# Second attention in pair steps, with half-array products and unpadded queries

## Chip, cores and metric

The kernel runs on one core of a Trainium2 chip. The metric is the device time of one launch in microseconds (us). TensorE is called PE, VectorE DVE, ScalarE ACT, GpSimd POOL and SyncE SP, as the profile calls them; PEld is PE's weight load.

## The reference, cut to what matters

Two layers run over 544 tokens: a prompt of 512 and a sample of 32 new tokens with a cache of 256. In each layer:

```
h = rms_norm(x, norm1)
a_q, a_k, a_v, b_q, b_k, b_v, i_q, i_k, i_w = split(h @ w_in)
o_a = stick_breaking(a_q, a_k, a_v)                      # 8 heads of 64, strictly causal
b_q = rms_norm(b_q, q_norm); b_k = rms_norm(b_k, k_norm) # per head
# keys of each query: the top k of an indexer's scores (i_q, i_k, i_w)
logits = b_q @ b_k^T / 8 + bias[pos]; not selected: -inf
o_b = softmax(logits) @ b_v                              # 8 heads of 64
x = x + concat(o_a, o_b) @ w_out
x = x + conv_ffn(rms_norm(x, norm2))
```

All in float32. For the 512 prompt queries the second attention works in tiles: a tile is one head and one block of 128 queries (b = 0 to 3), with 128(b + 1) keys.

## The kernel before

Activations lie transposed in SBUF, with 128 features of a matrix on the partitions and the 544 tokens along the row, so a column block of 128 of `w_in` is a *unit*, and a unit of the second attention holds two heads (a *pair* p = 0 to 3): head 2p on partitions 0 to 63, head 2p+1 on 64 to 127. A projection of a unit, `("G", kind, p, half)`, is cut into two halves of 24 products each (L1148, L1149, L1152: high and low parts of both operands). Its result stands in PSUM in one of two slots that are used in turn, and the next but one user of the slots waits until DVE or ACT has emptied it.

All engines walk one list of steps, made by `layer_steps`, `a_phase` and `b_phase`, and each engine takes from a step what is its own, in order. The names: G a half projection; E its result scaled and stored by DVE; S, N, Y, M, W the root-mean-square norm of bq and bk (ACT squares, PE adds over a head, DVE stores the mean, ACT does a logarithm and an exponential, DVE three operations and the write of q or k); T a transpose back to rows for an output; C the split of the next weights (ACT copies the high part, L868, POOL subtracts for the low part, L1660); TOPK one round of the top-k on DVE; IDX the indexer; AZ, AP, AS, AX, AW the first attention for one head; ASZ to ASV the same for the sample; O the split of an attention output for `w_out`.

The second attention (`b_phase`) takes 34 tiles one by one, head after head, then two of the sample. For tile i:

- BL: PE forms the logits in bank i % 2 of `a_ps` (L1341) and adds the mask of excluded keys by a product with the identity (L1342). It waits until ACT has read tile i-2. DVE adds the bias and takes the maximum (L1637), and negates it (L1639).
- BX: ACT takes the exponential and the sum (L1001).
- In the next BL: DVE takes the reciprocal (L1643), POOL scales the tile (L1674).
- BT: PE turns the tile by 128 x 128 blocks (L1351), ACT copies it out (L1017, L1019). All tiles use bank 2, so each waits for the copy of the one before.
- BV: after both heads of a pair, PE multiplies by the values (L672) into bank 3, and DVE copies to `o_t`.

The half projections and norms of the next pair stand between these steps by the table in `b_phase`, in some steps two, in many none.

A query is stored twice over in `q_pad`: for each head of the pair all 128 partitions, those of the other head being zero, so that a product with the pair's keys on 128 partitions gives one head. The writes are two DVE operations on 64 partitions each (L1464 for bq, L1488 for iq and aq). The indexer alone takes its products from 64 partitions (L1225). The last value unit, bv 3, is projected and turned at the end of the first attention.

Of the kernel before, what the change touches and what calls it, by code (L numbers as in the profile page):

```python
# [36 lines left out]
P = 128  # L37
# [81 lines left out]
B_TILES = [(h, b) for h in range(NH) for b in range(QB)] + [("s", 0), ("s", 1)]  # L119


def a_phase():
# [33 lines left out]
    bq, bk, bv = product("bq", 0), product("bk", 0), product("bv", 3)  # L156
    s += [("AZ", 6), ("AP", 6), ("AW", 2)] + turn + [bq[0], bq[1], ("E", "bq", 0), ("S", "bq", 0), ("AS", 6), ("AX", 6)]
    s += [("N", "bq", 0), ("Y", "bq", 0), bk[0], ("M", "bq", 0), ("W", "bq", 0), ("AZ", 7), ("AP", 7), bk[1], bv[0]]
    s += [("E", "bk", 0), ("S", "bk", 0), ("TOPK", 1), ("AS", 7), ("AX", 7), ("N", "bk", 0), ("Y", "bk", 0), ("TOPK", 1)]
    s += [("ASZ",), ("AW", 3), bv[1], ("ASP",), ("E", "bv", 3), ("ASS",), ("M", "bk", 0), ("W", "bk", 0), product("bq", 1)[0], ("ASV",), ("T", "bv", 3)]  # L160
# [3 lines left out]
def b_phase():  # L164

    extra = {i: [] for i in range(len(B_TILES) + 2)}
    late = {i: [] for i in range(len(B_TILES) + 2)}
    for p in range(1, PAIRS):  # L170
        i = 2 * QB * (p - 1) - 1
        halves = product("bq", p)
        if p > 1:
            late[i - 1] += [halves[0]]
        extra[i + 1] += [halves[1], ("E", "bq", p)]
        late[i + 1] += [("S", "bq", p)]
        late[i + 2] += [("N", "bq", p)]
        halves = product("bk", p)
        extra[i + 3] += [halves[0], ("Y", "bq", p)]
        extra[i + 3] += [("M", "bq", p)]  # L180
        extra[i + 4] += [("W", "bq", p), halves[1], ("E", "bk", p)]
        late[i + 4] += [("S", "bk", p)]
        late[i + 5] += [("N", "bk", p)]
        extra[i + 6] += [("Y", "bk", p)]
        extra[i + 6] += [("M", "bk", p)]
        extra[i + 7] += [("W", "bk", p)]
        extra[i + 8] += [("T", "bk", p)]
    extra[1] += [("T", "bk", 0)]
    n = len(B_TILES)
    for i in range(9):  # L190
        late[2 * i + 1] += [("TOPK", 1)]
    for j in range(KT // 2):
        extra[25 + j] += [("O", j)]
    extra[n - 1] += [("G", "wo", 0, 0)]
    extra[n] += [("G", "wo", 1, 0)]
    s = []
    for i in range(n + 2):
        if i <= n:
            s += [("BL", i)]
        s += extra[i]  # L200
        if i >= 3 and B_TILES[i - 3][1] == QB - 1 and B_TILES[i - 3][0] % 2:
            s += [("BV", B_TILES[i - 3][0] // 2)]
        if i >= 2:
            s += [("BT", i - 2)]
# [1514 lines left out]
```

## Time and profile before

| what | value |
|---|---|
| median of 3 runs | 1718.21 us (1717.36 to 1719.4) |
| the profiled execution's own time | 1717.34 us |
| its span, first to last instruction | 1715.5 us |
| mean granted PE clock | 0.982 of full |
| PE busy | 1606.1 us, 94% |
| DVE / ACT / POOL busy | 986.9 / 685.5 / 640.8 us (58% / 40% / 37%) |

Per layer, the second attention takes from 294.6 to 418.7 us in the first layer and from 1128.4 to 1252.5 us in the second.

PE's products are pipelined: the printed duration of one contains its way through the array, so that what a product costs in a row of them is the distance between two starts. Float32 products go in two passes, so one product shows as x2.

### The profile page before, as it was taken

What the parts mean: (1) busy time and instruction counts of PE and PEld (TensorE: products, weight loads), DVE (VectorE), ACT (ScalarE), POOL (GpSimd) and SP (SyncE); (2) the same over time, 40 slices, a digit from 0 to 9 for tenths busy, and PEclk for the clock granted to TensorE, in tenths of its full rate; (3) what the DMA queues carried; (4) which work ended last, traced back from release to release, by engine and by line L of the source; (5) the groups of instructions that cost most, each with busy time, mean ns of one, the idle gap of its engine ahead of it and who ended that gap; (6) DMA issues with size and microseconds to landing.
All of it is one profiled execution on the core that took longest, in us unless ns stands there. A gap on an engine that the chain in (4) does not pass through costs nothing.

```text
span 1715.5 us, 29957 instructions
## 1 busy us (share of the span) xinstructions
PE 1606.1 (94%) x11762; PEld 1475.9 (86%) x11762; DVE 986.9 (58%) x1823; ACT 685.5 (40%) x1296; POOL 640.8 (37%) x346
## 2 busy tenths in 40 slices
PE   5899999888999999999989899988789999999998
PEld 4678887666999999999987888876589999999998
DVE  6566766763756436616766666666556661663361
ACT  3333454444344324414433245534434441442342
POOL 4223331332734433433552323223345334434332
PEclk9899999998999999999999999999989999999999
DMA  6222212110322223233233231121012333333323
GB/s 184 68 78 82 70 50 64 51 50 1 89 85 87 87 87 87 87 89 91 74 89 98 65 96 48 47 70 51 20 50 78 95 87 87 87 87 87 86 82 97
DMA packets 242179, 131.43 MB, mean 77 GB/s; under 512 B 10303, under 2 KB 236591, under 8 KB 242039
## 3 DMA queue, kind: packets, MB, share of 16 engines
q1 hardware_dynamic: 242038, 129.52, 26.6%
q8 instruction: 93, 1.52, 0.4%
q14 instruction: 48, 0.39, 0.1%
HBM read 117.59 MB, written 11.62 MB: 75 GB/s over the span
## 4 chain that ended last, share of the span: by engine, by line
PE 70%; DVE 14%; ACT 6%; issue 3%; DVEq 3%; POOL 2%; ACTq 1%; DMA 0%; SPq 0%
PE g_ps L1148 13%; PE g_ps L1149 12%; PE g_ps L1152 12%; PE a_ps L1149 7%; PE a_ps L1148 7%; PE a_ps L1152 7%; DVE score L718 1%; ACT work L961 1%; PE a_ps L672 1%; POOL w_lo L1660 1%; PE a_ps L1238 1%; DVE score L1582 1%; DVE top L715 1%; PE a_ps L1225 1%; PE g_ps L1187 1%
## 5 line engine op out<-in xcount | busy, mean ns | idle before, releaser
L1660 POOL TENSOR_TENSOR w_lo<-raw,w_hi 128x1024 fp32r<-128x1024 f32 (+2 forms) x210 | 504.4, 2402 | 780.7 <-ACT w_hi L868 780.7
L1148 PE MATMUL g_ps<-h_hi,w_hi 128*128 128x272 f32 (+1 forms) x1632 | 454.0, 296 | 17.1 <-DVEq L1541 11.2
L1149 PE MATMUL g_ps<-h_lo,w_hi 128*128 128x272 f32 (+1 forms) x1632 | 443.6, 290 | 0.0
L868 ACT ACTIVATE w_hi<-raw 128x1024 fp32r<-128x1024 f32 (+2 forms) x210 | 217.4, 1035 | 502.9 <-PE g_ps L1152 371.2
L1152 PE MATMUL g_ps<-h_hi,w_lo 128*128 128x272 f32 (+1 forms) x1632 | 340.3, 290 | 0.0
L1148 PEld LDWEIGHTS g_ps<-h_hi,w_hi 128*128 128x128 f32 (+1 forms) x1632 | 309.1, 189 | 30.9 <-DVEq L1541 12.7
L1149 PEld LDWEIGHTS g_ps<-h_lo,w_hi 128*128 128x128 f32 (+1 forms) x1632 | 308.8, 189 | 0.9 <-issue 0.5
L1550 DVE SCALAR_TENSOR_TENSOR wts<-work,par,wts 128x546 f32<-128x546 f32 x176 | 201.2, 1143 | 100.0 <-ACT wts L1043 92.5
L1152 PEld LDWEIGHTS g_ps<-h_hi,w_lo 128*128 128x128 f32 (+1 forms) x1632 | 256.7, 189 | 0.0
L1148 PE MATMUL a_ps<-h_hi,w_hi 128*128 128x272 f32 x704 | 190.4, 288 | 0.0
L1149 PE MATMUL a_ps<-h_lo,w_hi 128*128 128x272 f32 x704 | 190.1, 288 | 0.0
L1152 PE MATMUL a_ps<-h_hi,w_lo 128*128 128x272 f32 x704 | 146.0, 288 | 0.0
L1148 PEld LDWEIGHTS a_ps<-h_hi,w_hi 128*128 128x128 f32 x704 | 132.6, 188 | 0.0
L1149 PEld LDWEIGHTS a_ps<-h_lo,w_hi 128*128 128x128 f32 x704 | 132.4, 188 | 0.0
L1152 PEld LDWEIGHTS a_ps<-h_hi,w_lo 128*128 128x128 f32 x704 | 110.0, 188 | 0.0
L1148 PE MATMUL g_ps<-act_hi,w_hi 128*128 128x272 f32 x364 | 99.3, 291 | 5.1 <-DVEq L1563 3.7
L1043 ACT ACTIVATE wts<-work,par 128x546 f32<-128x546 f32 x88 | 74.4, 845 | 61.1 <-DVEq L627 59.0
L1149 PE MATMUL g_ps<-act_lo,w_hi 128*128 128x272 f32 x364 | 98.2, 289 | 0.0
L1674 POOL TENSOR_SCALAR prob<-prob,stat 128x128 f32<-128x128 f32 (+2 forms) x68 | 47.8, 703 | 121.3 <-DVE stat L1643 121.3
L1148 PE MATMUL a_ps<-act_hi,w_hi 128*128 128x272 f32 x340 | 92.2, 289 | 0.9 <-POOL w_lo L1660 0.9
L1149 PE MATMUL a_ps<-act_lo,w_hi 128*128 128x272 f32 x340 | 91.7, 289 | 0.0
L1527 DVE TENSOR_TENSOR x_t<-x_t,g_ps 128x544 f32<-128x544 f32 x41 | 29.6, 721 | 107.4 <-PE g_ps L1152 106.7
(245 smaller groups left out, 2887.2 us busy)
## 6 DMA issues: line engine op xcount, KB each, us to landing
raw<-in_w_up SPq DMA_DIRECT2D x88, 512.0 KB, 3.8
raw<-in_w_in SPq DMA_DIRECT2D x56, 512.0 KB, 3.9
raw<-in_w_down SPq DMA_DIRECT2D x32, 512.0 KB, 3.7
raw<-in_w_out SPq DMA_DIRECT2D x16, 512.0 KB, 3.8
raw<-in_w_down SPq DMA_DIRECT2D x16, 384.0 KB, 3.4
x_nat<-in_x_prompt SPq DMA_DIRECT2D x4, 512.0 KB, 6.4
strip<-bias_line SPq DMA_DIRECT2D x8, 256.0 KB
out_p_av<-v_nat SPq DMA_DIRECT2D x4, 512.0 KB, 5.5
```

The lines of the kernel that those rows point to most:

```text
L672: mm = pe.matmul(a_ps[3][d, c * P:SEQ], v_nat[:, c, p * P + e * HD:p * P + (e + 1) * HD], pair_weights(w, e, c), start=(c == 0), stop=(c = ...
L715: dve.max(top8[0:n, i, :], s)
L718: dve.match_replace(s, top8[0:n, i, :], s, TAKEN)
L868: act.activation(w_hi[:, n % SPLIT, 0:kt, 0:c], raw[:, n % RAW, 0:kt, 0:c], ACT.Copy).then_inc(hi_done, 1)
L1043: act.activation(cbuf[kind], ubuf[kind][:, 2:U], ACT.Identity, bias=par[:, 3, col:col + 1], scale=par[:, 2, col:col + 1]).then_inc(c_tap.s ...
L1148: pe.matmul(g[0:c, a, 0:HALF], w_hi[:, s, j, 0:c], xh[:, mov], start=(j == 0), stop=False)
L1149: pe.matmul(g[0:c, a, 0:HALF], w_hi[:, s, j, 0:c], xl[:, mov], start=False, stop=False)
L1152: mm = pe.matmul(g[0:c, a, 0:HALF], w_lo[:, s, j, 0:c], xh[:, mov], start=False, stop=(j == kt - 1))
L1527: dve.tensor_tensor(halves(x_t[:, m, :]), halves(x_t[:, m, :]), g, ALU.add)
L1550: dve.scalar_tensor_tensor(c, u[:, tap:tap + U - 2], par[:, tap, col:col + 1], c, ALU.mult, ALU.add)
L1660: pool.tensor_tensor(w_lo[:, s, 0:kt, 0:c], raw[:, n % RAW, 0:kt, 0:c], w_hi[:, s, 0:kt, 0:c].bitcast(F32), ALU.subtract).then_inc(lo_done, 1)
L1674: pool.tensor_scalar(prob[:, i % 2, 0:w], prob[:, i % 2, 0:w], stat[:, i % 4, 3:4], 1.0, ALU.mult, ALU.mult).then_inc(b_nrm.sem, 1)
```

## The change

- `B_TILES` is ordered pair, block, head, and `b_phase` takes two tiles (both heads of a pair, one block) in a step: 16 prompt steps and one for the sample, plus one that ends it. One step holds at most one half projection.
- BL issues both heads' products from 64 partitions each, one behind the other (head 2p from the lower, head 2p+1 from the upper half of the array), then both masks. It waits until ACT has read both tiles of the step before.
- The reciprocal is one DVE operation for two tiles, in a step BR of its own, which POOL's two scalings follow.
- BT of a step turns both tiles behind the projection of the next step. Small tiles (b < 2) share bank 2 of `a_ps`; of large ones the first takes bank 2 and the second bank 3. `prob` has four tiles.
- `q_pad` is replaced by `q_t`, without zeros: one DVE operation on 128 partitions in place of two on 64. AZ reads 64 partitions and issues its four masks behind its four products.
- The projection of bv 3 and its turn move from the end of the first attention to steps 11 to 13 of the second. In their place stand the second half of bq 1, its E and S, and the first half of bk 1.

```diff
-B_TILES = [(h, b) for h in range(NH) for b in range(QB)] + [("s", 0), ("s", 1)]
+B_TILES = [(2 * p + e, b) for p in range(PAIRS) for b in range(QB) for e in range(2)] + [("s", 0), ("s", 1)]
...
-    s += [("ASZ",), ("AW", 3), bv[1], ("ASP",), ("E", "bv", 3), ("ASS",), ("M", "bk", 0), ("W", "bk", 0), product("bq", 1)[0], ("ASV",), ("T", "bv", 3)]
+    s += [("ASZ",), ("AW", 3), bq1[1], ("ASP",), ("ASS",), ("M", "bk", 0), ("W", "bk", 0), ("E", "bq", 1), ("S", "bq", 1), product("bk", 1)[0], ("ASV",)]
...
+    for q in range(PAIRS - 1):
+        p, j = q + 1, QB * q
+        k = product("bk", p)
+        first[j] += [("N", "bq", p), ("BR", j), ("Y", "bq", p), ("M", "bq", p)]
+        half[j] += [k[0]] if q else []
+        after[j] += [("W", "bq", p)]
+        first[j + 1] += [("BR", j + 1)]
+        half[j + 1] += [k[1], ("E", "bk", p)]
+        after[j + 1] += [("S", "bk", p)]
+        first[j + 2] += [("N", "bk", p), ("BR", j + 2), ("Y", "bk", p), ("M", "bk", p)]
+        first[j + 3] += [("T", "bk", p - 1), ("BR", j + 3), ("W", "bk", p)]
+        if p < PAIRS - 1:
+            later = product("bq", p + 1)
+            half[j + 2] += [later[0]]
+            half[j + 3] += [later[1], ("E", "bq", p + 1)]
+            after[j + 3] += [("S", "bq", p + 1)]
...
+    half[last - 1] += [value[0]]
+    half[last] += [value[1], ("E", "bv", PAIRS - 1)]
+    first[last] += [("T", "bk", PAIRS - 1)]
+    first[last + 1] += [("T", "bv", PAIRS - 1)]
+    half[last + 1] += [("G", "wo", 0, 0)]
+    half[last + 3] += [("G", "wo", 1, 0)]
+    for j in range(last, n):
+        first[j] += [("BR", j)]
+    for j in range(9):
+        after[j] += [("TOPK", 1)]
     for j in range(KT // 2):
-        extra[25 + j] += [("O", j)]
+        after[9 + j // 2] += [("O", j)]
     s = []
-    for i in range(n + 2):
...
+    for j in range(n + 1):
+        if j < n:
+            s += [("BL", j), ("BX", 2 * j), ("BX", 2 * j + 1)]
+        s += first[j] + half[j]
+        if j >= 2 and B_TILES[2 * j - 4][1] == QB - 1:
+            s += [("BV", (j - 2) // QB)]
+        if j:
+            s += [("BT", 2 * j - 2), ("BT", 2 * j - 1)]
+        s += after[j]
     s += [("BV", "s")]
...
-        q_pad = sb("q_pad", [P, 2, 2, TOK])
+        q_t = sb("q_t", [P, 2, TOK])
...
-                    ks = k_t[:, k_slot("ak", p), :]
+                    r = slice(e * HD, (e + 1) * HD)
+                    ks, q = k_t[r, k_slot("ak", p), :], q_t[r, q_slot("aq", p), :]
...
+                        for e in range(2):
+                            r = slice(e * HD, (e + 1) * HD)
+                            pe.matmul(a_ps[e][:, 0:w], q_t[r, q_slot("bq", p), b * P:(b + 1) * P], k_t[r, k_slot("bk", p), 0:w], start=True, stop=False)
+                        for e in range(2):
+                            pe.matmul(a_ps[e][:, 0:w], ident_b, excl[:, WOFF[b]:WOFF[b] + w], start=False, stop=True).then_inc(bl_full.sem, 1)
...
-                        for e in range(2):
-                            r = slice(e * HD, (e + 1) * HD)
-                            dve.scalar_tensor_tensor(halves(q_pad[r, q_slot(kind, p), e, :]), g[r], HD ** -0.5, halves(rstd[r, :]), ALU.mult, ALU.mult)
+                        dve.scalar_tensor_tensor(halves(q_t[:, q_slot(kind, p), :]), g, HD ** -0.5, halves(rstd[:]), ALU.mult, ALU.mult)
...
+                elif k == "BR":
+                    j = st[1]
+                    dve.wait_ge(b_exp.sem, b_exp.at(l, btiles[2 * j + 1]))
+                    c = 2 * (j % 2)
+                    dve.reciprocal(stat[:, c:c + 2, 3:4], stat[:, c:c + 2, 2:3]).then_inc(b_rcp.sem, 1)
```

First place: PE at the seam of the two attentions. Before, from the end of the sample's running sums (L1306) on: the first half of bq 1, the sample's values (L1314), the turn of bv 3 (L1198), and the first tile of the second attention (L1341).

```order
L1306 MATMUL a_ps<-work,cr 32x256
L1148 MATMUL g_ps<-h_hi,w_hi 128x272 [waits lo_done,g_free1]
...
L1314 MATMUL a_ps<-wts,vsa 128x64 [waits o_out,a_w]
L1314 MATMUL a_ps<-wts,vsa 128x64 x11
L1198 MATMUL g_ps<-cf,o_t 128x128 [waits e_done,g_free0]
...
L1341 MATMUL a_ps<-k_t,q_pad 128x128 [waits r_done,a_w]
L1342 MATMUL a_ps<-excl,cb 128x128
```

Now, in the changed program (L1315 is the old L1306, L1154 a projection, here the first half of bk 1, L1323 the sample's values, L1352 and L1354 the products and masks of a tile, L1193 the norm's product):

```order
L1315 MATMUL a_ps<-work,cr 32x256
L1154 MATMUL g_ps<-h_hi,w_hi 128x272 [waits lo_done,g_free1]
...
L1323 MATMUL a_ps<-wts,vsa 128x64 [waits o_out,a_w]
L1323 MATMUL a_ps<-wts,vsa 128x64 x11
L1352 MATMUL a_ps<-k_t,q_t 128x128 [waits r_done,a_w]
L1352 MATMUL a_ps<-k_t,q_t 128x128
L1354 MATMUL a_ps<-excl,cb 128x128 x2
L1193 MATMUL g_ps<-sq,cf 128x272 [waits sq_done,g_free0]
```

The turn of bv 3 has left; the wait on `g_free1` was for the emptying of bv 3 and is now for that of bq 1, which DVE does behind M and W of bk 0.

Second place: DVE in step 4, the first of the second group of four steps (L1647 and L1649 are the maximum with its read-out and the negation, L1435 N, L1654 the reciprocals, L1463 to L1470 M, L1479 and L1487 W of bq 2, L719 and L722 a round of the top-k).

```order
L1647 ISA a_ps,stat<-a_ps,strip 128x128 [waits b_nrm,bl_full]
L1647 ISA stat 128x1
L1649 TENSOR_SCALAR stat<-stat 128x1
...
L1435 TENSOR_SCALAR va<-g_ps 128x544 [waits g_full]
L1654 RECIPROCAL stat<-stat 128x2 [waits b_exp]
L1463 SCALAR_TENSOR_TENSOR va<-va,vb 128x544 [waits y_done]
L1465 TENSOR_TENSOR va<-va,vb 128x544
L1470 SCALAR_TENSOR_TENSOR vb<-va,vb 128x544
L1479 SCALAR_TENSOR_TENSOR q_t<-nraw,qk_gain,vb 128x544 [waits bl_full]
L1487 COPY q_smp<-q_t 64x32 x2
L719 MAX top<-score 32x8
L722 MATCH_REPLACE score<-top,score 32x288
```

Both tiles' maxima now come first in a step, and everything for the norms and the top-k stands behind the reciprocals, which wait for the exponentials of the same step.

## Rows read from the trace of the kernel before

**Rows 1.** The page: the span in 40 slices, tenths PE was busy, and its granted clock.
```profile
PE   5899999888999999999989899988789999999998
...
PEclk9899999998999999999999999999989999999999
```

**Rows 2.** Stages of layer 0: us, each engine's busy us (instructions), clock, DMA share, GB/s.
```profile
294.60:322.40 27.80, 23.41 (x153) 19.06 (x152) 19.57 (x57) 12.83 (x33) 9.01 (x8) 1.00 0.30 89
322.40:352.90 30.50, 25.93 (x172) 20.43 (x171) 21.37 (x62) 13.99 (x37) 9.86 (x10) 1.00 0.15 45
352.90:383.00 30.10, 23.80 (x148) 18.06 (x146) 19.77 (x58) 14.00 (x37) 10.58 (x11) 0.95 0.16 45
383.00:418.70 35.70, 30.93 (x172) 20.93 (x171) 11.99 (x48) 14.90 (x46) 8.04 (x12) 0.88 0.03 9
```

**Rows 3.** Timeline (start us, us, engine line op): a full-array tile; the indexer's half-array products.
```profile
305.21 1.02 PE L1341 MATMUL a_ps<-k_t,q_pad 128*128 128x512 f32 x2
306.07 0.38 PE L1342 MATMUL a_ps<-excl,cb 128*128 128x512 bf16 x1
...
74.09 1.13 PE L1225 MATMUL a_ps<-ik_t,q_pad 64*128 64x512 f32 x4 [0.47 <-ACT prob L953]
```

**Rows 4.** Timeline, PE: full array, half array, full array again.
```profile
71.92 0.41 PE L1152 MATMUL g_ps<-h_hi,w_lo 128*128 128x272 f32 x2
72.27 1.35 PE L1225 MATMUL a_ps<-ik_t,q_pad 64*128 64x256 f32 x8
...
75.15 0.68 PE L1225 MATMUL a_ps<-iks_t,q_pad 64*32 64x288 f32 x4
75.75 0.39 PE L1148 MATMUL g_ps<-h_hi,w_hi 128*128 128x272 f32 x1
```

**Rows 5.** Timeline, PE: AZ for a head, its first product and mask, and what follows.
```profile
159.31 1.02 PE L1238 MATMUL a_ps<-q_pad,k_t 128*128 128x512 f32 x2
160.16 0.22 PE L1239 MATMUL a_ps<-cb 128*128 128x128 bf16 x1
...
161.82 0.37 PE L1148 MATMUL g_ps<-h_hi,w_hi 128*128 128x272 f32 x1
```

**Rows 6.** Timeline, PE and DVE: the seam of the two attentions.
```profile
286.61 0.61 PE L1306 MATMUL a_ps<-work,cr 32*32 32x256 f32 x2
...
284.54 2.59 DVE L1446 SCALAR_TENSOR_TENSOR va<-va,vb 128x544 f32<-128x544 f32 x1 [0.28 <-issue]
...
289.77 0.18 DVE L1477 COPY ksb_t<-k_t 128x32 f32<-128x32 f32 x1
```

**Rows 7.** Timeline, DVE: a top-k round, two maxima, the write of a query pair.
```profile
302.41 0.45 DVE L715 MAX8 top<-score 32x8 f32<-32x288 f32 x1 [0.21 <-issue]
...
303.56 0.57 DVE L1637 CUSTOM_DVE_ANT_0 a_ps<-a_ps,strip 128x384 f32<-128x384 f32 x1
...
306.94 0.70 DVE L1637 CUSTOM_DVE_ANT_0 a_ps<-a_ps,strip 128x512 f32<-128x512 f32 x1
...
307.92 1.79 DVE L1464 SCALAR_TENSOR_TENSOR q_pad<-nraw,qk_gain,vb 64x544 f32<-64x544 f32 x2
```

**Rows 8.** Timeline, DVE and ACT: an operation of M, a weight copy, an exponential.
```profile
346.28 0.72 DVE L1446 SCALAR_TENSOR_TENSOR va<-va,vb 128x544 f32<-128x544 f32 x1 [0.36 <-ACT vb L904]
...
340.20 1.06 ACT L868 ACTIVATE w_hi<-raw 128x1024 fp32r<-128x1024 f32 x1 [3.31 <-PE g_ps L1152]
...
341.43 0.68 ACT L1001 ACTIVATE prob<-a_ps,stat 128x512 f32<-128x512 f32 x1
```

**Rows 9.** Timeline, DVE: a query write of the indexer.
```profile
59.18 1.46 DVE L1488 SCALAR_TENSOR_TENSOR q_pad<-g_ps,rstd 64x544 f32<-64x544 f32 x2 [7.04 <-PE g_ps L1152]
```

**Rows 10.** Timeline, PE: a turn at either clock, and the last values of the sample.
```profile
352.08 0.63 PE L1198 MATMUL g_ps<-cf,k_t 128*128 128x128 f32 x4 [0.68 <-DVEq L1478]
...
381.48 1.09 PE L1198 MATMUL g_ps<-cf,k_t 128*128 128x128 f32 x4 [2.34 <-DVEq L1478]
...
412.88 5.76 PE L1365 MATMUL a_ps<-wts,vsb 128*128 128x64 f32 x24 [0.62 <-ACT wts L1010]
```

More of the change, by code:

```diff
@@ L169, in b_phase @@
[L169 to L191, printed above, removed]
+    n = len(B_TILES) // 2
+    first, half, after = ({j: [] for j in range(n + 1)} for _ in range(3))
+    for q in range(PAIRS - 1):
[14 more added lines that the diff above has]
+            after[j + 3] += [("S", "bq", p + 1)]
@@ L192, in b_phase @@
+    last = QB * (PAIRS - 1)
+    value = product("bv", PAIRS - 1)
+    half[last - 1] += [value[0]]
[8 more added lines that the diff above has]
+        after[j] += [("TOPK", 1)]
     for j in range(KT // 2):
-        extra[25 + j] += [("O", j)]
@@ L1224, in _ @@
                             keys = ik_t[r, 0:w] if b < QB else iks_t[r, 0:w]
-                            pe.matmul(a_ps[i % 4][0:nq, 0:w], q_pad[r, q_slot("iq", p), e, q0:q0 + nq], keys, start=True, stop=True).then_inc(i_full.sem, 1)
+                            pe.matmul(a_ps[i % 4][0:nq, 0:w], q_t[r, q_slot("iq", p), q0:q0 + nq], keys, start=True, stop=True).then_inc(i_full.sem, 1)
                 elif k == "AZ":
@@ new lines, in _ @@
+                    if pair[0][0] == "s":
+                        pe.wait_ge(kc_done.sem, kc_done.at(l, "b"))
+                        pe.wait_ge(tk_done.sem, tk_done.at(l, "s"))
+                        for half in range(2):
+                            z = a_ps[half][:, 0:w]
+                            for r in range(2):
+                                p = 2 * half + r
+                                pe.matmul(z[r * 64:(r + 1) * 64, :], q_smp[:, p, :, :], ks_t["b"][:, p, :], start=True, stop=False, skip_group_check=True)
+                            pe.matmul(z, rep_b[0:DEC, :], excl_s[:], start=False, stop=True, skip_group_check=True).then_inc(bl_full.sem, 1)
+                    else:
+                        p = pair[0][0] // 2
+                        if b == 0:
+                            pe.wait_ge(r_done.sem, r_done.at(l, ("bk", p)))
+                        for e in range(2):
[3 more added lines that the diff above has]
+                            pe.matmul(a_ps[e][:, 0:w], ident_b, excl[:, WOFF[b]:WOFF[b] + w], start=False, stop=True).then_inc(bl_full.sem, 1)
@@ L1374, in _ @@
             dve.tensor_copy(cr[:], cr_f32)
-            dve.memset(q_pad[:], 0.0)
             dve.memset(q_smp[:], 0.0)
@@ L1471, in _ @@
                                 r = slice(e * HD, (e + 1) * HD)
-                                dve.tensor_copy(q_smp[r, pair, e, :], q_pad[r, q_slot("bq", pair), e, SEQ:TOK])
+                                dve.tensor_copy(q_smp[r, pair, e, :], q_t[r, q_slot("bq", pair), SEQ:TOK])
                     else:
```

130 lines of the change are left out of this document (54 added, 76 removed).

## The prediction

> **What bounds the kernel now.** I read the page first: PE is the busiest engine, with nines and eights nearly all through, and its clock is full but for a few slices [rows 1]. So time is lost or won either in PE's own work or where PE waits. Then I cut the second attention of layer 0 into four stages, one for each pair of heads, by the start of their first tiles [rows 2]; layer 1 goes the same way. They take 27.8, 30.5, 30.1 and 35.7 us, 124.1 in all, and PE is busy 23.4, 25.9, 23.8 and 30.9 of them: about 20 us of a layer PE does nothing. DVE is at 60 to 70% in the first three. No engine is full; each tile's chain (PE, DVE, ACT, DVE, POOL, PE, ACT) meets in-order queues. The feed-forward part is untouched and stays.
>
> **PE's own work in a tile.** A full-array product of 512 columns and its mask are 0.86 us apart in start [rows 3]: two passes of 0.43. The indexer's two half-array products of 512 columns, four passes, last 1.13 us from first start to last end; of that 0.27 is the way through the array, so they too cost 0.86 [rows 3]. Both halves together cost what one full product costs. A head's products over its four blocks take 0.86 x (1 + 3/4 + 1/2 + 1/4) = 2.15 us, so a pair saves 2.15. Against it stand changes between full and half array: the last full pass of 272 columns should end its stream at 72.16 and the half array starts at 72.27; the other way the stream should end near 75.63 and the full array starts at 75.75 [rows 4]. That is 0.11 a change, two in each step, 0.9 in four. Net 1.3 a pair, **5.2 a layer of PE work**. But little of this is time by itself, since the stages are not PE-bound.
>
> The page TensorEngine Tiling (Array Packing) of the Trainium skill, section Key Properties, speaks against this change: a switch of tiling mode drains the engine. By that rule, the trace agrees in kind, and its rows put the price at 0.11 us.
>
> **First attention (AZ).** A head alone works on one half, so nothing overlaps; the product block takes 2.51 us until the projection behind it [rows 5]. The same passes remain (2.15), four masks in a row at about 0.06 to 0.1 each, and two changes at 0.11: 2.6 to 2.75. I take +0.1 a head, **+0.8 a layer**; the ends are 0 and +0.25 a head.
>
> **Query writes.** Two operations on 64 partitions take 1.46 us [rows 9]; an operation on the full 128 takes 0.72 [rows 8]. PE waits at the end of this write in four places of a layer (three of the indexer, one before the first keys), in one of them only 0.3 us long: 3 x 0.73 + 0.3 = **-2.5 a layer**. The zeroing of `q_pad` at the start lies beside DMA and PE work before the first tokens and counts nothing; without that cover it would be worth under 0.4.
>
> **The seam.** This is a new wait. The product of half bk 1 needs the slot that bq 1 holds, and DVE empties it behind M and W of bk 0, which end at 289.95 [rows 6], plus 0.8 for E: 290.8. Before, a half projection started on PE at 287.2, behind L1306 [rows 6]. PE stands still for 3.6 us. Behind it in PE's queue are the sample's values and the first tiles. The turn of bv 3 (0.63) [rows 10] is gone from here: **+3.0 a layer**. That M's first operation takes 2.59 instead of 0.72 [rows 6, 8] is POOL's subtraction beside it, which stays where it is, so DVE gains nothing from E of bv 3 having left.
>
> **The second attention, step by step.** I walk PE, DVE and ACT through the 17 steps. DVE per tile: 0.98 us for 512 keys and 0.84 for 384, negation and reciprocal included [rows 7], so 0.70 and 0.57 for the others, 6.2 for a group of four steps. N and E of two norms: 4 x 0.8, 3.2. M: three operations at 0.8 [rows 8], twice, 4.8. Writes: q falls from 1.79 to 0.9 [rows 7] plus 0.4 of copies; k 1.15. Value copy 0.9. Top-k round 302.41 to 303.56, 1.15 [rows 7], four of them. That is 22.2. Now the waits, since the reciprocal stands in the queue between maxima and the rest: M waits for a logarithm and an exponential over 544 columns, 0.7 each by the exponential of 512 [rows 8], so 1.4 twice; the other two steps wait 0.7 for the last exponential. Sum 26.4 us, where PE has 25.9 - 1.3 = 24.6. So **DVE's queue bounds group 2: 26.4** for 30.5.
> Group 1 lacks the value copy and one wait for a square: 24.6 for 27.8. In it DVE holds N, M, W and a round of step 0 before the maxima of step 1, so PE, which has one half projection there, stands still for about 5 us.
> Group 3 has one round and four O operations (3.0) and no projection in step 10: there and in step 11 PE waits about 3 us for DVE. 28.3 for 30.1.
> Group 4 takes over half a projection of bv 3 and two turns (3.0 + 0.65 + 0.65). PE-bound to the last tile pair (three half projections at 3.0, values 2.4, two turns 1.3, tiles 4.1, their turning 1.6, waits 2.6: 21 us), then a bare chain with no projection: two sample tiles of 288 keys 1.5, eight turns 0.9 (0.63 for five [rows 10]), ACT's copies behind two exponentials 2.4 at 0.4 to 0.7 each, values 2.4 (the columns of a pair's products, 2.15, and two changes) to 4.6 by the clock, a last turn that waits for DVE's copy out of bank 3 (0.7 and two handshakes, 1.3), a copy 0.9, the last values 5.8 [rows 10]; 15.2 to 17.4, I take 16.5. 37.5 for 35.7.
> Sum 116.8 for 124.1: **-7.3 a layer**. Costed at nothing: POOL's scalings in pairs (PE turns a tile behind a half projection, 3 us of cover; without it, in steps 10, 14 and 16, under 1.5 us, counted), and v's output DMAs, now later but over 20 us before their reader.
>
> **Clock.** A turn takes 0.63 us at the full level of 2.4 GHz and 1.09 at 1.2 GHz, after some 2.3 us of standing and a thin stretch before it [rows 10]; stage 3 was granted 0.95 [rows 2]. New stretches of 3.6 and 5 us invite that: **+1.0 a layer**, between 0 and 3.
>
> **Sum.** 2 x (0.8 - 2.5 + 3.0 - 7.3 + 1.0) = -10.0. The profiled execution took 1717.3 us, 0.9 under the median of the runs. On its own time 1707.3; on the median **1708**. About 0.2% (3.4 us) is what a measurement tells from no change.
>
> **Rivals.**
> (a) The walk holds without clock losses or slack, AZ at nothing, and values in full clock: 2 x (-2.5 + 3.0 - 9.5) = -18: 1700. For it: DVE sums are made with stretched operations. Chance 0.15.
> (b) The halves do not overlap in the tiles, since each is a different head: no 2.15 a pair, 17 us of PE work in both layers back. Two thirds lie under DVE's queue, 6 come through: 1714. Against it: the indexer does it with the same form [rows 3]. Chance 0.07.
> (c) Handshakes eat what the walk frees: each of 17 steps costs 0.25 us more than counted, 8.5 in both layers: 1716 to 1717, no change. For it: my walk leaves PE idle for 1.8 us of group 2 where it was for 4.6 before. Chance 0.11.
> (d) **Slower.** ACT's queue takes the place: behind a unit's end it holds a weight copy (1.06), two tile copies and a square (each under 0.7, by the exponential's size) [rows 8] ahead of the next step's exponentials, and with only one step in flight PE's next tiles need both of these exponentials. If 0.65 us a step shows on top, it is 11 us a layer: 2 x (-5.0 + 11) = +12: 1730. It decides from 0.3 us a step. Against it: these copies end before DVE's two maxima do in most steps. Chance 0.08.
> (e) Half-array passes on the same rows do not hide their weight loads. In the indexer each half ran its second pass straight behind its first, four passes in 0.86 [rows 3], so this is nearly excluded. If it were so, a pass would wait some 0.11 us, as at a change, which hides no load either [rows 4]: eight passes for each of 16 heads in AZ 14 us, two in each of 32 steps 7: 1708 + 21 = 1729. Chance 0.02. The Trainium skill's page TensorE: Matmul & The Clock Gate, Part 3, says that loads overlap running products only when the row group differs; the trace differs.
>
> **How the numbers follow.** The forecast has 0.57; its own width, bounds of the clock and of AZ, lets 0.03 of it fall within 0.2% of no change. Faster by over 0.2%: 0.54, (a) 0.15 and 0.05 of (b), 0.74. Same: (c) 0.11, 0.03, and 0.02 of (b), 0.16. Slower: (d) and (e), 0.10. The range starts at 1697, a little under (a), and reaches to 1719, above (c); outside it are (d), (e) and a tail of (a).
>
> **What would show it.** In the changed profile: products of a pair in 0.43 us a pass with both halves started together; a PE wait of 3.6 us on DVE before bk 1's first half; groups of about 24.6, 26.4, 28.3 and 37.5 us; a wait of about 5 us on an exponential in step 1; query writes of 0.72; AZ 2.6 to 2.7. I am wrong if the groups take over 28 us, or if the seam shows no wait.

## Result and the profile after

The changed kernel took **1703.4 us** (median of 4 runs, 1700.2 to 1705.3) where the kernel before took 1717.8 in the same session (1713.9 to 1719.4): ratio **0.9924**, 95% interval 0.9902 to 0.9946. The forecast was 1708 with a range of 1697 to 1719: the sign and the total were right. Two of its terms were not, as the experiments below show, and that their errors cancelled was luck.

The profiled execution of the changed kernel took 1700.2 us, with a span of 1698.4. The page, in the lines of [rows 1] and with PE's busy time:

```profile
PE 1593.1 (94%) x11762; PEld 1472.4 (87%) x11762; DVE 969.3 (57%) x1764; ACT 686.5 (40%) x1296; POOL 630.1 (37%) x346
...
PE   6899998878999999999999999979799999999998
...
PEclk9899999988999999999999999989999999999999
```

Lines have moved: the products of a pair step are L1352, its masks L1354, AZ's products L1245, the write of a key pair L1490. The four groups of pair steps of layer 0, against [rows 2] (length and each engine's busy us with its instructions, granted clock, DMA share, GB/s):

```profile
290.88:316.84 25.96, 19.67 (x122) 15.40 (x122) 18.74 (x55) 11.50 (x29) 6.49 (x9) 0.87 0.08 21
316.84:344.61 27.77, 23.99 (x170) 19.19 (x170) 20.18 (x56) 14.25 (x37) 9.28 (x11) 1.00 0.18 49
344.61:375.47 30.86, 23.78 (x145) 18.36 (x146) 21.20 (x55) 16.49 (x42) 9.26 (x11) 0.89 0.15 44
375.47:411.67 36.20, 31.79 (x206) 23.53 (x206) 9.96 (x38) 13.57 (x44) 7.97 (x12) 0.92 0.20 62
```

They take 120.8 us where 124.1 stood and 116.8 was forecast. In layer 1 the four groups take 119.7 where 126.2 stood (from the first tile at 1126.4 us, not at 1128.4 as the part on the time before has it). PE is busy 99.2 of the 120.8, so it still stands still for 21.6, about as long as before (20). The waits are long ones now, in a few places (timeline of PE, layer 0; in brackets the idle time ahead of the row and its releaser):

```profile
282.56 0.39 PE L1154 MATMUL g_ps<-h_hi,w_hi 128*128 128x272 f32 x1 [2.90 <-DVEq L1554]
...
302.31 1.65 PE L1352 MATMUL a_ps<-k_t,q_t 64*128 64x384 f32 x4 [4.59 <-ACT prob L1005]
...
344.61 0.80 PE L1352 MATMUL a_ps<-k_t,q_t 64*128 64x128 f32 x4 [2.80 <-DVEq L1493]
...
365.65 0.70 PE L1352 MATMUL a_ps<-k_t,q_t 64*128 64x512 f32 x2 [2.58 <-ACT prob L1005]
365.65 1.13 PE L1352 MATMUL a_ps<-k_t,q_t 64*128 64x512 f32 x4 [2.58 <-ACT prob L1005]
...
375.47 0.80 PE L1352 MATMUL a_ps<-k_t,q_t 64*128 64x128 f32 x4 [3.92 <-DVEq L1493]
```

The first is the seam (bk 1's half behind the write of bq 1), the second the exponentials of step 1. The two on L1493 are at the first step of a pair: TensorE has nothing to do until DVE has written the key pair. 1.65 for four passes of 384 at 302.31, where 0.92 is the length elsewhere, is the lower clock after a wait. The two rows at 365.65 are the same product, its first two passes and all four. The waits of layer 1 are at the same places, with 2.89, 4.74, 2.55, 2.58 and 2.19 us.

Where the 17 us of the two profiled executions went is read from the starts of the same products in both (us; length of the stretch, layer 0 / layer 1):

| from, to | before | after |
|---|---|---|
| indexer's first product (layer 1: the first norm's sums), first AZ | 79.8 / 90.4 | 75.0 / 85.0 |
| first AZ, sample values of attention a | 148.9 / 149.7 | 152.8 / 152.9 |
| from there to the next norm (second attention and output projection) | 182.7 / 187.0 | 179.8 / 177.7 |

So 10.2 us of the 17 come ahead of the first attention, in the indexer's stage, for which the forecast had 4.4 (three writes a layer at 0.73). The start of the program up to the first indexer product took between 55.8 and 61.6 us over all these profiles, also among kernels that do the same there; a few us of any single profile are of that kind, so I judge kernels by their medians.

### The profile page after: what moved, and what is told of

It is laid out like the page before. It is cut to its first block, busy times and chain, and to the rows that moved or that the text cites. A ratio compares the mean times of both kernels' runs of the same rounds, so it can differ in the third digit from the quotient of the medians.

```text
span 1698.4 us, 29872 instructions
## 1 busy us (share of the span) xinstructions
PE 1593.1 (94%) x11762; PEld 1472.4 (87%) x11762; DVE 969.3 (57%) x1764; ACT 686.5 (40%) x1296; POOL 630.1 (37%) x346
## 4 chain that ended last, share of the span: by engine, by line
PE 68%; DVE 15%; ACT 6%; issue 3%; DVEq 3%; POOL 2%; ACTq 1%; DMA 0%; SPq 0%
PE g_ps L1154 13%; PE g_ps L1155 12%; PE g_ps L1158 12%; PE a_ps L1155 7%; PE a_ps L1154 7%; PE a_ps L1158 7%; DVE score L722 1%; ACT work L965 1%; PE a_ps L1245 1%; POOL w_lo L1671 1%; DVE a_ps L1647 1%; DVE top L719 1%; PE a_ps L676 1%; DVE score L1595 1%; DVE va L1465 1%
## 5 line engine op out<-in xcount | busy, mean ns | idle before, releaser
L1154 PE MATMUL g_ps<-h_hi,w_hi 128*128 128x272 f32 (+1 forms) x1632 | 458.4, 298 | 16.8 <-DVEq L1554 11.9
L1154 PEld LDWEIGHTS g_ps<-h_hi,w_hi 128*128 128x128 f32 (+1 forms) x1632 | 312.4, 191 | 26.9 <-DVEq L1554 14.1
L1154 PE MATMUL a_ps<-h_hi,w_hi 128*128 128x272 f32 x704 | 190.4, 288 | 0.0
L1154 PEld LDWEIGHTS a_ps<-h_hi,w_hi 128*128 128x128 f32 x704 | 132.6, 188 | 0.0
L1154 PE MATMUL g_ps<-act_hi,w_hi 128*128 128x272 f32 x364 | 99.4, 291 | 5.1 <-DVEq L1576 3.7
L1685 POOL TENSOR_SCALAR prob<-prob,stat 128x128 f32<-128x128 f32 (+4 forms) x68 | 38.1, 572 | 173.7 <-DVE stat L1654 173.7
L1154 PE MATMUL a_ps<-act_hi,w_hi 128*128 128x272 f32 x340 | 92.3, 289 | 0.9 <-POOL w_lo L1671 0.9
L1155 PE MATMUL a_ps<-act_lo,w_hi 128*128 128x272 f32 x340 | 91.8, 288 | 0.0
```

The costliest lines, as they stand in the source:

```text
L1154: pe.matmul(g[0:c, a, 0:HALF], w_hi[:, s, j, 0:c], xh[:, mov], start=(j == 0), stop=False)
L1155: pe.matmul(g[0:c, a, 0:HALF], w_hi[:, s, j, 0:c], xl[:, mov], start=False, stop=False)
L1685: pool.tensor_scalar(prob[:, i % 4, 0:w], prob[:, i % 4, 0:w], stat[:, i % 4, 3:4], 1.0, ALU.mult, ALU.mult).then_inc(b_nrm.sem, 1)
```

## Experiments

Each kernel was timed against the kernel before in five rounds. "Against the changed kernel" is the quotient of the two ratios, with its interval from both. All edits are to the changed kernel unless said otherwise.

### The queries alone, and the queries of the first half alone

`unpad_only` is the kernel before with the new queries everywhere. `front_unpadded` has them in the indexer and the first attention, and leaves the second attention's padded.

```diff
-q_pad = sb("q_pad", [P, 2, 2, TOK])
+q_t = sb("q_t", [P, 2, TOK])
...
-pe.matmul(z, q_pad[:, q_slot("bq", p), e, b * P:(b + 1) * P], k_t[:, k_slot("bk", p), 0:w], ...)
+pe.matmul(z, q_t[r, q_slot("bq", p), b * P:(b + 1) * P], k_t[r, k_slot("bk", p), 0:w], ...)
```

(the last two lines in `unpad_only` alone. In both, the masks of AZ stand behind its products, as in the changed kernel.)

> The kernel before with the unpadded queries alone (query tensor of 128 rows, one write for each pair, indexer, first attention and second attention reading half arrays; single tiles, orders and seam as before). Terms of the prediction: per layer AZ +0.8 and writes -2.5, so -3.4 in both layers, about 1714.3 us (-0.2%). What the two traces suggest: all that lies ahead of the seam is 7.6 us shorter in layer 0 and 11.4 us in both, so about 1706 us (-0.65%), with the query copies behind the aq write at 0.36 us and not 2.23. By this second theory the pair steps and the seam together are worth only 2 to 4 us.

> The kernel before with unpadded queries in the indexer and the first attention alone; the second attention's queries stay padded (two writes of which one is 128 rows), its tiles read full arrays, single tiles, seam as before. Theory A (the half arrays cost the single tiles of the second attention 10 to 12 us a layer, and the eight unpadded writes with their copies gain all that the changed kernel gained ahead of the seam): -13 to -17 us against before, about 1700. Theory B (the loss behind the seam in the run with the queries alone is the granted clock of the last group, which any earlier arrival brings): the last group again at a clock of 0.7 and about 43 us, and the total near 1715.

Measured: `unpad_only` 1722.1 against 1716.0, ratio **1.0039** [1.0024, 1.0053]: slower. `front_unpadded` 1703.5 against 1718.3, ratio **0.9919** [0.9893, 0.9946]: as fast as the whole change. Both expectations of the first run missed its sign; of the second, theory A held.

Two things follow. The queries ahead of the seam are worth about 14 us, four times what the forecast gave them, and the whole of what the change brings. And half arrays in the second attention's single tiles cost 1.2%, 20 us, although `unpad_only` has eight writes fewer there; at the price found below these are 6 us, so the half arrays cost some 26. From the first tile to the sample's logits in layer 0, the two kernels show (windows of `front_unpadded`, then of `unpad_only`):

```profile
288.78:396.91 108.13, 89.90 (x527) 67.18 (x526) 69.31 (x209) 51.32 (x136) 35.46 (x36) 0.93 0.17 51
```

```profile
289.18:405.76 116.58, 104.11 (x526) 68.77 (x525) 67.05 (x206) 51.27 (x136) 35.95 (x36) 0.88 0.16 47
...
382.43:428.59 46.16, 42.71 (x172) 25.29 (x171) 12.12 (x49) 15.07 (x46) 8.30 (x12) 0.66 0.03 7
```

DVE has three instructions less, ACT and POOL do the same work; PE is busy 14 us longer at a lower clock. What a tile costs is read from starts, not from printed lengths. These are a tile of 512 with the half array, its second pass by itself, and then the same tile with the full array, each with the pass ahead of it:

```profile
317.09 0.41 PE L1152 MATMUL g_ps<-h_hi,w_lo 128*128 128x272 f32 x2
317.43 1.12 PE L1345 MATMUL a_ps<-k_t,q_t 64*128 64x512 f32 x2
318.49 0.39 PE L1346 MATMUL a_ps<-excl,cb 128*128 128x512 bf16 x1
```

```profile
317.97 0.59 PE L1345 MATMUL a_ps<-k_t,q_t 64*128 64x512 f32 x1
```

```profile
315.68 0.42 PE L1153 MATMUL g_ps<-h_hi,w_lo 128*128 128x272 f32 x2
315.93 1.02 PE L1345 MATMUL a_ps<-k_t,q_pad 128*128 128x512 f32 x2
316.79 0.38 PE L1346 MATMUL a_ps<-excl,cb 128*128 128x512 bf16 x1
```

The half-array tile starts 0.34 us behind the row ahead of it where the full one starts 0.25 behind, and its mask starts 1.06 behind it where the full one's starts 0.86. Of these 0.20 us, 0.11 lie between its two passes (0.53 to 0.54 us apart, where full passes are 0.43 apart) and 0.09 between the second pass and the mask. That is 0.3 us a tile, and the same at every width: medians of 0.42, 0.63, 0.84 and 1.06 us from product to mask for 128 to 512 columns, against 0.22, 0.43, 0.65 and 0.86. In 32 tiles it is 9.5 us a layer and 19 in both. The clock comes on top. Between two levels, a granted mean of 0.88 over 116.6 us is 28 us at the lower one (2 x 0.12 x 116.6), and 0.93 over 108.1 is 15; half the difference, 6, is lost, if PE is busy in it. Its last group took 46.2 us at 0.66; in `front_unpadded` that group took 38.1 at 0.82. Taken to the sample's last values in both layers, the tiles' 19 us and the clock's 26 by the same arithmetic are more than the 26 between the two profiled executions there (276.1 for 249.8), so part of either lies in waits. How the 26 divide is open, and so is why the clock fell: the runs with pair steps below, half or full, don't differ in it.

### The writes split again

```diff
-dve.scalar_tensor_tensor(q_t[:, q_slot("bq", p), :], nraw[:], qk_gain[:, 0:1], vb[:], ...)
+for e in range(2):
+    r = slice(e * HD, (e + 1) * HD)
+    dve.scalar_tensor_tensor(q_t[r, q_slot("bq", p), :], nraw[r, :], qk_gain[r, 0:1], vb[r, :], ...)
```

and the same for iq and aq.

> The changed kernel with each query write put back into two operations of 64 rows, everything else as changed. Terms of the prediction: 4 waits in a layer end later by 0.73 us, so +5 to +6 us, about 1709 (+0.3% over the changed kernel). What the traces suggest: 12 writes in a layer and the copies stretched again behind the aq write (2.2 us), +9 to +12 us, about 1714.

Measured: ratio 1.0026 [1.0012, 1.0040]; against the changed kernel +1.0% (0.26 either way), **+17.5 us** (4.4 either way) for 24 writes in both layers with the copies behind them, 0.73 for each write on average. The second theory was nearer, and still short: far more than four of twelve writes are on the path. Half of the 22.5 us between the two profiled executions lies again in the indexer's stage, which took 79.6 us in layer 0 and 91.8 in layer 1, much as before the change.

The average hides that one write brings more than itself and two bring nothing. These are DVE's and POOL's timelines at the write of aq 0, in the kernel before, the changed one, and the one with split writes:

```profile
124.78 1.46 DVE L1488 SCALAR_TENSOR_TENSOR q_pad<-g_ps,rstd 64x544 f32<-64x544 f32 x2 [4.73 <-PE g_ps L1152]
126.31 2.23 DVE L1496 COPY q_smp<-q_pad 64x32 f32<-64x32 f32 x2
...
125.97 2.34 POOL L1660 TENSOR_TENSOR w_lo<-raw,w_hi 128x1024 fp32r<-128x1024 f32 x1 [9.11 <-ACT w_hi L868]
```

```profile
120.45 0.72 DVE L1501 SCALAR_TENSOR_TENSOR q_t<-g_ps,rstd 128x544 f32<-128x544 f32 x1 [4.72 <-PE g_ps L1158]
121.25 0.36 DVE L1509 COPY q_smp<-q_t 64x32 f32<-64x32 f32 x2
...
121.64 2.40 POOL L1671 TENSOR_TENSOR w_lo<-raw,w_hi 128x1024 fp32r<-128x1024 f32 x1 [9.11 <-ACT w_hi L872]
```

```profile
122.26 1.46 DVE L1505 SCALAR_TENSOR_TENSOR q_t<-g_ps,rstd 64x544 f32<-64x544 f32 x2 [4.73 <-PE g_ps L1158]
123.79 2.23 DVE L1513 COPY q_smp<-q_t 64x32 f32<-64x32 f32 x2
...
123.45 2.34 POOL L1675 TENSOR_TENSOR w_lo<-raw,w_hi 128x1024 fp32r<-128x1024 f32 x1 [9.11 <-ACT w_hi L872]
```

POOL's subtraction starts 1.19 us behind the write's start in all three. With one short write the two small copies are over before it; with two they start inside it and take 2.23 us for 0.36. In the kernel before the first of the two copies took 2.04 of the 2.23 and ended at 128.35, POOL's operation at 128.31: it had waited for it. The Trainium skill's page SBUF — State Buffer, section Who interferes with whom, says that a DVE copy can take a mode in which it contends with GpSimd for a shared pair of ports, and that whoever issues first holds the pair for the whole of its instruction while the other is blocked; by that rule the trace agrees. Writing one operation less shortened this place by 2.6 us, 0.73 of it the write. This and the two indexer writes inside the stage, at 0.73 each, are 4.1 of the 4.85 us that the stage lost in layer 0; the rest may be the clock, granted 0.98 before and 1.00 after.

At aq 1 and aq 3 it goes the other way. POOL's subtraction already runs when the first copy starts, so a write that ends earlier only makes the copy wait longer. At aq 1 (the changed kernel, then split writes):

```profile
145.46 0.72 DVE L1501 SCALAR_TENSOR_TENSOR q_t<-g_ps,rstd 128x544 f32<-128x544 f32 x1
146.25 2.44 DVE L1509 COPY q_smp<-q_t 64x32 f32<-64x32 f32 x2
```

```profile
149.83 1.45 DVE L1505 SCALAR_TENSOR_TENSOR q_t<-g_ps,rstd 64x544 f32<-64x544 f32 x2
151.36 1.71 DVE L1513 COPY q_smp<-q_t 64x32 f32<-64x32 f32 x2
```

They take 3.23 and 3.24 us from the write's start to the copies' end. So the changed kernel's queue on DVE is shorter by 2.6 us at aq 0, by nothing at aq 1 and aq 3, and by 0.73 to 0.79 at each of the other nine writes of a layer: 9.4 us, and 8.8 a layer (2.2 either way) came out as time.

### Masks between the products

```diff
 for e in range(2):
     pe.matmul(a_ps[e][:, 0:w], q_t[r, ...], k_t[r, ...], start=True, stop=False)
-for e in range(2):
     pe.matmul(a_ps[e][:, 0:w], ident_b, excl[...], start=False, stop=True)
```

> The changed kernel with the order product, mask, product, mask in each pair step, so that the two half arrays never work together and each step has four changes of the array's form. By the prediction's rival (halves apart) +6 us, about 1709. If TensorE is not what bounds the groups of pair steps: the step's first maximum starts earlier (its mask ends before the second product), so 0 to +2 us.

Measured: ratio 0.9975 [0.9961, 0.9989], against the changed kernel +0.5% (0.26), about **+9 us**. It is the forecast's rival (b) brought about, priced there at +6, with two more changes of the array's form in each step. A step of 512 keys in this kernel, and then in the changed one:

```profile
312.45 1.12 PE L1352 MATMUL a_ps<-k_t,q_t 64*128 64x512 f32 x2
313.50 0.39 PE L1353 MATMUL a_ps<-excl,cb 128*128 128x512 bf16 x1
313.82 1.12 PE L1352 MATMUL a_ps<-k_t,q_t 64*128 64x512 f32 x2
314.88 0.39 PE L1353 MATMUL a_ps<-excl,cb 128*128 128x512 bf16 x1
```

```profile
335.93 1.13 PE L1352 MATMUL a_ps<-k_t,q_t 64*128 64x512 f32 x4
336.99 0.60 PE L1354 MATMUL a_ps<-excl,cb 128*128 128x512 bf16 x2
```

2.82 us from first start to last end there, 1.66 here: two heads on two halves take 1.13, and one alone 1.12. The halves work at the same time. The change of the array's form shows here too: from a mask's start to the next product there are 0.32 us, where a second mask follows the first at 0.21 (0.60 for two, 0.39 for one), so 0.11, as the forecast had it. The Trainium skill's page TensorEngine Tiling (Array Packing), section Key Properties, says that a switch drains the engine; by that rule the trace agrees. But it is not the whole price: as in the single tiles above, the first passes behind the change stand 0.11 further from the second ones, and the mask 0.09 further from these, so a block of half-array products costs 0.3 us more than its passes. By the medians of these distances the order product, mask, product, mask takes TensorE 3.3 us more a pair, 27 in both layers, and a third of that came out as time.

### Full arrays in the pair steps

`pairs_full` has padded queries and full-array products in the pair steps, everything ahead of the seam unpadded. `combo_full` has the same on top of both edits of the next part.

```diff
-pe.matmul(a_ps[e][:, 0:w], q_t[r, q_slot("bq", p), b * P:(b + 1) * P], k_t[r, ...], ...)
+pe.matmul(a_ps[e][:, 0:w], q_pad[:, q_slot("bq", p), e, b * P:(b + 1) * P], k_t[:, ...], ...)
```

> The changed kernel with padded queries and full arrays in the second attention's pair steps alone (first attention and indexer unpadded; each bq write is two operations, one of 128 rows; the third and fourth probability slot lie in the first attention's sample values; all orders as changed). The logits of a full group of four pair steps take TensorE about 2 us more, the four writes 0.73 us each. Theory A (half arrays together lower the granted clock of the second attention as they do alone, 17 us a layer at the lower clock where 6 stand in the kernel before): the group's clock rises, -5 us a layer for it, +3 for the writes, and the longer logits lie in waits: about 1700. Theory B (two halves side by side are what the pair step gains, the clock falls with any wait of TensorE): +4 to +8 us in all, about 1710.

> The same full arrays under the kernel with both edits (half projection in the first pair step, key write ahead of the reciprocal), which took 1688.8. Theory A: -2 to -4 us, about 1685. Theory B: +4 to +8, about 1695; with fewer waits to lie in, the longer logits count more than in the run without the two edits.

Measured: 0.9985 [0.9972, 0.9998] and 0.9895 [0.9877, 0.9913]: +0.6% (0.26) against the changed kernel and +0.7% (0.3) against the same kernel with half arrays, 10 and 11 us. Theory B held in both. Both have eight second writes, 5.8 us at the average price of the split writes, so some 5 us are the logits themselves; the two runs agree, but each has an interval of 4 us or more. Both also keep two of the four tiles of `prob` elsewhere, since the padded queries take the room; that this costs nothing is not shown. Theory A fell: in `pairs_full` the stretch from the first step to the sample's logits was granted 0.91 in layer 0, in the changed kernel 0.92.

```profile
292.23:404.75 112.52, 94.37 (x575) 74.74 (x578) 71.63 (x199) 51.83 (x136) 31.67 (x38) 0.91 0.17 49
```

### The waits in the seam and at the head of a pair

`bk1_in_step0` takes the half projection out of the seam; `w_first` writes the key pair ahead of the reciprocal; `combo` does both.

```diff
-... ("E", "bq", 1), ("S", "bq", 1), product("bk", 1)[0], ("ASV",)]
+... ("E", "bq", 1), ("S", "bq", 1), ("ASV",)]
...
-half[j] += [k[0]] if q else []
+half[j] += [k[0]]
...
-first[j + 3] += [("T", "bk", p - 1), ("BR", j + 3), ("W", "bk", p)]
+first[j + 3] += [("T", "bk", p - 1), ("W", "bk", p), ("BR", j + 3)]
```

> The changed kernel with the first half of projection bk 1 taken from ahead of the sample value product and put behind the logits of the second attention's first pair step, as the later pairs have it. The wait of 3.7 us on the write of bq 1 should go, and the half projection should lie in the wait of 4.6 us that TensorE has on the exponentials of step 1. If both hold, -8 us a layer, about 1687. If DVE's queue holds step 1 up whatever TensorE does, the half projection is hidden and only the seam gains or the other way round: -3.7 us a layer, about 1696. If the wait only moves to the sample value product, which waits for the sample's weights: no change, 1703.

> The changed kernel with the write of key pair p put ahead of the reciprocal in the pair step before its first use. TensorE waits 0.8, 2.8 and 3.9 us in layer 0 for that write. If DVE's queue is the cause, each wait shrinks by the time the write stood behind the exponentials and the reciprocal (1 to 2 us each), -3 to -5 us a layer, about 1695. If the wait is on the exponentials in truth, or comes back on the normalization that starts later, 0 to -1 us, about 1703.

> Both edits together: the first half of projection bk 1 in the second attention's first step, and the key write ahead of the reciprocal. If they hold different waits the gains add: 1694.3 less 3 to 8, about 1688. If the later steps just take up what the first edit left, 1694.

Measured: 0.9871 [0.9857, 0.9886], 0.9888 [0.9865, 0.9911] and **0.9829** [0.9803, 0.9855]: 9, 6 and 16 us under the changed kernel. The effects add. `combo` took 1688.8 us, less than either kernel of the case. In it (PE, layer 0) the seam's wait is gone and step 1's is 1.85; at the first pair's head there is none, at the other two 1.1 each, but the waits on the squares behind the first two heads have grown to 1.6 and 2.3:

```profile
298.00 0.92 PE L1352 MATMUL a_ps<-k_t,q_t 64*128 64x384 f32 x4 [1.85 <-ACT prob L1005]
...
338.47 0.49 PE L1352 MATMUL a_ps<-k_t,q_t 64*128 64x128 f32 x4 [1.12 <-DVEq L1493]
...
341.48 2.15 PE L1193 MATMUL g_ps<-sq,cf 128*128 128x272 f32 x4 [2.30 <-ACT sq L899]
...
369.76 0.49 PE L1352 MATMUL a_ps<-k_t,q_t 64*128 64x128 f32 x4 [1.08 <-DVEq L1493]
```

The same place in the changed kernel, on DVE, shows why the order of two operations matters: the write waits for both exponentials by standing behind the reciprocal, though it needs neither.

```profile
373.83 0.17 DVE L1654 RECIPROCAL stat<-stat 128x2 f32<-128x2 f32 x1 [0.85 <-ACT prob L1005]
373.92 0.78 DVE L1490 SCALAR_TENSOR_TENSOR k_t<-nraw,qk_gain,vb 128x544 f32<-128x544 f32 x1
374.77 0.52 DVE L1492 COPY ksb_t<-k_t 128x32 f32<-128x32 f32 x1
```

### Two more moves on top

```diff
-for j in range(9):
+for j in (1, 1, 2, 3, 5, 5, 6, 7, 7):
     after[j] += [("TOPK", 1)]
```

> The same with the nine rounds of the sample's top-k moved from steps 0 to 8 into the steps where DVE has no key or query to norm (two in step 1, one in 2 and 3, two in 5, one in 6, two in 7). If DVE's queue sets steps 1 and the pair starts, -2 to -4 us more, about 1684. If the two rounds at once hold up the maxima of steps 2, 6 and 8, no gain or +2.

Measured: 0.9876 [0.9855, 0.9897], 8 us over `combo`. Step 1's wait fell to 0.56, but those at the heads of the pairs rose from 0, 1.12 and 1.08 to 1.57, 2.09 and 2.65. The rounds had cost less spread out.

`late_norm` puts the head sums of a query behind the half projection of its step:

```diff
-first[j] += [("N", "bq", p), ("BR", j), ("Y", "bq", p), ("M", "bq", p)]
-half[j] += [k[0]]
+norm = [("N", "bq", p), ("BR", j), ("Y", "bq", p), ("M", "bq", p)]
+first[j] += [norm.pop(1)] if q else norm
+half[j] += [k[0]] + (norm if q else [])
```

> The kernel with both edits, in which TensorE waits 1.6 us (second group) and 2.3 us (third group) in layer 0 on the squares of a query at the group's head, before the half projection that stands behind them. This edit puts the head sums, and DVE's norm of them, behind that half projection in those two groups, and the reciprocal ahead. If the half projection fills the waits: -3 to -4 us a layer, about 1682. If the norm that comes 6 us later pushes DVE's query write and top-k onto the next step's maxima, the wait moves to the exponentials: 1689 or a little more.

Measured: 0.9839 [0.9824, 0.9854], the same as `combo` within the intervals. The waits on the squares at the two heads are gone, and waits of 1.78 and 2.19 on exponentials have come in the step behind the next: the second of the two expectations.

### The last value projection ahead of the seam

On `combo`. The halves of bq 1 change place too, to either side of the sample's values, so both edits are measured together:

```diff
-... bk[1], bq1[0]]
+... bk[1], bv[0]]
...
-... ("ASZ",), ("AW", 3), bq1[1], ("ASP",), ("ASS",), ("M", "bk", 0), ("W", "bk", 0), ("E", "bq", 1), ("S", "bq", 1), ("ASV",)]
+... ("ASZ",), ("AW", 3), bv[1], ("ASP",), ("E", "bv", 3), ("ASS",), ("M", "bk", 0), ("W", "bk", 0), bq1[0], ("ASV",), ("T", "bv", 3), bq1[1], ("E", "bq", 1), ("S", "bq", 1)]
...
-half[last - 1] += [value[0]]
-half[last] += [value[1], ("E", "bv", PAIRS - 1)]
```

> The kernel with both edits, but the last value projection back ahead of the seam as in the kernel before, and the projection bq 1 around the sample value product. It brings 12.4 us of projection a layer out of the last steps. If those steps had waits to fill, they keep most of their length (36 us goes to about 30, as in the kernel before, whose last group took 35.7 at a low clock with 31 busy): +4 to +8 us a layer, 1697 to 1705. If the place of the projection doesn't matter: 1689.

Measured: 0.9883 [0.9864, 0.9902], +0.5% (0.3) or 9 us over `combo`, at the low end of what was expected. The third and fourth group of it, and then of `combo`:

```profile
345.87:375.59 29.72, 20.81 (x120) 15.21 (x122) 20.84 (x56) 16.39 (x41) 8.85 (x10) 0.86 0.16 45
375.59:410.91 35.32, 30.57 (x176) 21.67 (x177) 9.35 (x38) 13.25 (x44) 6.53 (x12) 0.84 0.06 17
```

```profile
338.47:369.76 31.29, 25.33 (x145) 19.09 (x146) 20.84 (x56) 16.51 (x41) 8.85 (x10) 0.84 0.15 43
369.76:404.61 34.85, 30.44 (x206) 22.30 (x206) 10.07 (x39) 14.83 (x47) 8.90 (x13) 0.96 0.20 64
```

The expectation has the projection's length wrong: two halves of 3.0 us are 6, not 12.4. With 55 instructions more, the two groups of `combo` are 1.1 us longer in layer 0 (66.1 for 65.0) and 3.2 in layer 1 (66.0 for 62.8). In the fourth of layer 0, PE is as long busy with 30 fewer instructions when the projection is missing, since it works at a lower clock. So the projection costs 1.1 and 3.2 of its 6 us where the change put it, and the 7.7 that are hidden in both layers are most of the 9 us. The rest may be the place of bq 1, which no run took alone.

## Why the forecast was right, and where it wasn't

The total was right by luck, because two terms missed in opposite directions. The queries (writes and AZ) were forecast at -3.4 us in both layers and brought -14; seam, second attention and clock were forecast at -6.6 and brought nothing that shows (0.9924 for the whole change, 0.9919 for the queries ahead of the seam alone). By the two profiled executions they are +6.8 us at the seam and -9.8 behind it, in both layers.

- **Query writes, "PE waits at the end of this write in four places", -2.5 a layer.** This step failed. `front_unpadded` alone gained 14 us in both layers, and putting all the second writes back cost 17.5, 8.8 a layer. The four places were read as the only ones because PE stands still there visibly. My reading is that a write elsewhere on the queue holds the next thing on DVE, and PE waits for that under another name; what the runs show is that of the 9.4 us a layer by which the split writes lengthen DVE's queue, 8.8 (2.2 either way) came out as time. The 1.9 us of copies that POOL's subtraction had stretched weren't in the sum at all: I took the copies as short from their size and didn't look at their row.
- **Second attention, -7.3 a layer.** This failed too: 120.8 for 124.1 us in layer 0, -3.3, and 119.7 for 126.2 in layer 1, -6.5. In layer 0 groups 1, 2 and 4 came within 1.4 us of the walk (26.0, 27.8 and 36.2 for 24.6, 26.4 and 37.5); group 3 took 30.9 for 28.3. In it PE waits 2.58 on exponentials and 3.92 on the key write at its end, 6.5 where the walk had 3. The walk put the key write in DVE's sum, and never asked what TensorE's next products wait for at a pair's head.
- **Seam, +3.0.** The wait was 2.90 on PE [the first row of the waits above] where 3.6 was forecast, and DVE's M, the cause, was stretched as before (2.79 for one operation). From the start of the first attention's last product (L1306, now L1315) to the first tile: 11.8 us for 7.9 before, +3.9 in layer 0 and +2.9 in layer 1, with the lower clock behind the wait in it. Mechanism and size held, and `bk1_in_step0` showed that it is worth undoing, together with step 1's wait: the forecast had that at 5 us, it was 4.59.
- **AZ, +0.8.** Right. 2.56 us from the first product to the projection behind it (2.51 before, [rows 5]), and the first product starts 0.22 us behind the pass ahead of it where it was 0.13: +0.13 a head, +1.0 a layer.

```profile
152.48 2.42 PE L1245 MATMUL a_ps<-q_t,k_t 64*128 64x512 f32 x8
154.83 0.40 PE L1248 MATMUL a_ps<-cb 128*128 128x128 bf16 x4
155.04 0.37 PE L1154 MATMUL g_ps<-h_hi,w_hi 128*128 128x272 f32 x1
```

- **Halves side by side at 0.43 a pass.** Half right. Both halves start and end together: 0.70 for the first two passes of a pair's product and 1.13 for all four. But the forecast took 0.27 of the 1.13 in [rows 3] for the way through the array. From first product to mask there are 1.06 us, not 0.86 + 0.11, because the second passes start 0.53 behind the first:

```profile
336.46 0.59 PE L1352 MATMUL a_ps<-k_t,q_t 64*128 64x512 f32 x2
```

  So a step's block costs 0.3 us beside its passes and not 0.22, and by the medians a pair saves 1.0 us of PE work, not 1.3. Rival (b) was rightly thin: a third of the work that `masks_between` adds came out, as the forecast had it (6 of 17; 9 of 27). Rival (e) holds for the first pass behind a change alone, with its 0.11; the next ones are 0.32 us apart at 384 columns in AZ, which hides the load.
- **Clock, +1.0.** Groups 1 and 3 were granted 0.87 and 0.89 for 1.00 and 0.95. By the two levels that is about 6.7 and 6.8 us at the lower one, for 0 and 3.0, and group 4 gained back 2.8; half of the net 7.7 is 3.8 in layer 0, if PE was busy all that time; in layer 1 it is some 2.5 by the same working. The term was mis-sized, and lies near its bound of 3.
- Rivals (a) and (d) didn't come. No queue of ACT's stood in the way: ahead of each step's first exponential ACT stood idle for 1.1 to 9.2 us, for DVE. Rival (c) came in size behind the seam: the second attention took 4.0 and 2.9 us longer than the walk, where (c) has 4.25 a layer. It was in a few long waits more than in each step, and what the queries gained hid it. The forecast said that groups over 28 us would make it wrong, and group 3 did go over, at 30.9 and 29.7.

What stays open: how the loss between `front_unpadded` and `unpad_only` divides between the tiles' lengths (9.5 us a layer from their starts) and the lower clock, since no run took the clock away alone.

## What to carry over

A second operation on a queue is priced by taking it out and putting it back, not by counting the places where another engine is seen waiting for it; here 24 of them cost 0.73 each on average, with the copies that they stretched or relieved. When halves of an array can work side by side, issue both before anything that needs the whole array, and price a block of half-array products from its starts, with what stands ahead of it and behind it: 0.3 us a block here. In pairs the halves gained some 5 us, and in single tiles they lost 20. And after a rebuild, read the long waits and ask of each whether the operation that ends it had to stand behind what is ahead of it in its queue; two edits of a line or two gave as much here as the whole change.

## What was not expected of the hardware

- Two DVE copies of 64x32 took 0.36 us alone, and 2.23 or 2.44 beside POOL's subtraction of 128x1024 (rows of aq 0 and aq 1 above).
- The first pass of a block of half-array products stood 0.53 us ahead of the second at 512 columns, where 0.43 is the distance of full-array passes.
- An operation of 128x544 in M took 2.79 us beside such a subtraction, 0.73 else.
- The last group was granted 0.92 in the changed kernel and 0.96 in `combo`, with the same 206 instructions, 0.84 in `bv3_early` and 0.66 in `unpad_only`. By the two levels the last is some 31 us at the lower one of 46.
